# A two-layer-block transformer kernel: 37 products of two constants taken out of TensorE's program at three borders between stages

## The chip, the cores and the metric

The kernel runs on one core of one Trainium2 chip. The metric is the device time of one execution in microseconds (us); the time of a kernel is the median of its runs.

## The reference

A first block (norm, chunked attention with relative positions beside a gated short convolution, gates, an MLP with squared ReLU) and then two layers of a second block. All of it is on 512 tokens of 1024 channels in float32. Cut to what the change touches:

```python
def rmsnorm(x, g):
    xf = x.astype(F32)
    y = xf * lax.rsqrt(jnp.mean(xf * xf, axis=-1, keepdims=True) + NORM_EPS)
    return (y * g.astype(F32)).astype(x.dtype)

for layer in range(DEPTH_2):                     # 2 layers
    u = rmsnorm(h, norm_g[layer, 0])
    ...
    y = mixer(u, mem_kv, ...)                    # window attention in layer 0, HGRN2 in layer 1
    h = h + rmsnorm(y, norm_g[layer, 1])
    f = conv_ffn(rmsnorm(h, norm_g[layer, 2]), ffn_w_in[layer], ffn_conv_w[layer],
                 ffn_conv_b[layer], ffn_w_out[layer])
    h = h + rmsnorm(f, norm_g[layer, 3])
```

The three borders are the places where `h + rmsnorm(y, ...)` of one product's output has to be complete before the next product can begin: after layer 0's mixer, after layer 0's `conv_ffn`, and after layer 1's mixer.

## The kernel before, in words

The program is written by hand, one instruction stream for each engine, with semaphores between them. Activations lie with channels on the partitions: 8 tiles of 128 channels, 512 tokens in the columns. Each matrix product is made of three products of parts ("three_passes", L604 to L606): weights and activations are split into a high and a low part (w_hi, w_lo, h_hi, h_lo), and high by high, low by high and high by low are added up in a PSUM bank of 512 columns. The weights stream from memory through a ring of 6 slots; GpSimd splits them.

A stage is one such matrix product (`STAGES` in the program): blocks of 128 output channels, each a sum over the stage's tiles of input channels. A stage with a "lead" runs its first four blocks side by side: step k takes input tile k into all four banks, 12 products with 512 columns a step, so it can begin as soon as the first tile of h is there. `lead_first` (L656, L657, L660) is step 0 of the two ffn_in stages and of b_in, with the four h_lo products put last; `lead_step` is each later step (L604 to L606).

The order of TensorE's work is the order in which the code calls it. Around a border this is `last_block`, for the last of the 8 output blocks of a_out, ffn_out0 and b_out:

- all tiles of the block but three; then the sum over channels of the squares of the seven earlier blocks (`square_sums`, L940, products with one column of the constant ones, into ps_t); then the last three tiles;
- ScalarE squares the last accumulator (L1358), `square_sums` adds it (L940), ScalarE takes the root (rms, L1368), VectorE the reciprocal (rstd, L1866);
- TensorE spreads rstd over the partitions with four products with the constant ident (L981, into ps_o);
- VectorE scales y with it and with the gain (L1871), adds it to x_res (L1882); ScalarE makes h_hi of tile 0 (L1373) and VectorE h_lo (L1837). The eight tiles follow each other, and the next stage's lead takes them in this order.

`turning` (L948) stands in the three holes of that sequence: products of the constants ones and ident, 128 by 128 in float32, into the bank that block 0 of the next stage will start afresh. Their result is used by nobody. `gain_rows` (L955) stands at the third border alone: eight products that lay the gain of the last norm along the rows, read by ScalarE.

```python
            def turning(st, count):
                bank_free(st, 0)
                for _ in range(count):
                    nc.tensor.matmul(banks[st.banks[0]][:, 0:P], const("ones"), const("ident"), start=True, stop=True)
```

Calls of `last_block`: from `mixer_out` with a_out (first border, next stage ffn_in0), from `conv_mlp(0)` with ffn_out0 (second, next b_in), from `mixer_out` with b_out (third, next ffn_in1).

Of the kernel before, what the change touches and what calls it, by code (L numbers as in the profile page):

```python
# [25 lines left out]
P = 128  # L26
# [160 lines left out]
def build(nc, stream, x_in, mem_in, consts_in, rope_in, params_in, masks_in, ext_in, out):  # L187
# [11 lines left out]
    with ExitStack() as ctx:  # L199
# [116 lines left out]
        def const(name, n=P):  # L316
            c = CONST_COLS[name]
            return consts[:, c:c + n]
# [31 lines left out]
        banks = [*acc, *ps_s, ps_o, ps_t]  # L350
# [233 lines left out]
        def _(pe):  # L584
# [3 lines left out]
            def out_free():  # L588

                if n["copied"]:  # L590
                    pe.wait_ge(o_copied, n["copied"])
                if n["o"]:
                    pe.wait_ge(o_taken, n["o"])

            def take_t(sem_, value):

                if t_free:
                    pe.wait_ge(*t_free[0])
                t_free[:] = [(sem_, value)]
# [10 lines left out]
            def bank_free(st, c):  # L610

                if st.before[c] is not None:
                    before, i = st.before[c]
                    pe.wait_ge(before.free, i + 1)
                elif st.name == "conv":
                    pe.wait_ge(stages["v1"].free, c + 3)
                elif st.name == "gate":
                    pe.wait_ge(s_used, n["unit"])
                elif c == BANKS and st.name not in ("a_out", "b_out"):
                    pe.wait_ge(s_used, n["unit"])  # L620
                    out_free()
# [51 lines left out]
            def block_tiles(st, first, end, x_hi, x_lo, cols=T, done=1):  # L673

                for tile in range(first, end):
                    c, k = divmod(tile, st.kt)
                    if k == 0:
                        bank_free(st, c)
                    if tile % SLOT_TILES == 0:
                        pe.wait_ge(split_made, st.first_slot + tile // SLOT_TILES + 1)  # L680
                    three_passes(st, banks[st.banks[c]][:, 0:cols], (st.first_slot + tile // SLOT_TILES) % RING,
                                 tile % SLOT_TILES, x_hi, x_lo, k, cols, done)
# [240 lines left out]
            st = stages["proj"]  # L923
# [13 lines left out]
            def square_sums(src, last):  # L937

                for b in range(BLOCKS):
                    mm = nc.tensor.matmul(ps_t[:, b:b + 1], src[:, b * P:(b + 1) * P], const("ones")[:, 0:1],  # L940
                                          start=False, stop=last and b == BLOCKS - 1)
                return mm

            def turning(st, count):

                bank_free(st, 0)
                for _ in range(count):
                    nc.tensor.matmul(banks[st.banks[0]][:, 0:P], const("ones"), const("ident"), start=True, stop=True)  # L948

            def gain_rows(then, half):  # L950

                lead_block = GAIN_LEADS[half]
                bank_free(then, lead_block)
                for i in range(DT // 2):
                    mm = nc.tensor.matmul(banks[then.banks[lead_block]][:, i * P:(i + 1) * P],  # L955
                                          param("norm_g", 56 + half * DT // 2 + i).to_broadcast([P, P]), const("ident"), start=True, stop=True)
                mm.then_inc(gain_made, 1)

            def last_block(st, x_hi, x_lo, sq, then):

                tiles = st.cbs * st.kt
                block_tiles(st, tiles - st.kt, tiles - 3, x_hi, x_lo)
                n["rms"] += 1
                n["y"] += 1
                take_t(rms_ready, n["rms"])
                pe.wait_ge(y_sq_used, (DT - 2) * n["y"])
                nc.tensor.matmul(ps_t[:, 0:BLOCKS], const("ones"), small["zero"][:].to_broadcast([P, BLOCKS]), start=True, stop=False)
                square_sums(rstd_in, False)
                block_tiles(st, tiles - 3, tiles, x_hi, x_lo)
                if then.name == "ffn_in1":  # L970
                    gain_rows(then, 0)
                else:
                    turning(then, 4)
                pe.wait_ge(y_sq, DT * n["y"])
                square_sums(sq[:, (DT - 1) % 2, :], True).then_inc(y_sum, 1)

                turning(then, 2)
                out_free()
                pe.wait_ge(rms_used, n["rms"])
                for b in range(BLOCKS):  # L980
                    mm = nc.tensor.matmul(ps_o[:, b * P:(b + 1) * P], rstd[:, b:b + 1].to_broadcast([P, P]), const("ident"),  # L981
                                          start=True, stop=True)
                mm.then_inc(y_rstd, 1)
                if then.name == "ffn_in1":
                    gain_rows(then, 1)
                    turning(then, 5)
                else:
                    turning(then, 9)
                n["o"] += 1

            def last_slot(st, s, blocks):
# [48 lines left out]
            def conv_mlp(layer):  # L1040
                st = stages[f"ffn_in{layer}"]
                lead(st, h_hi, h_lo, waits_for(h_ready, n["h"]), halves=4 + 2 * layer)
                block_at(st, BANKS, h_hi, h_lo)
                block_tiles(st, (BANKS + 1) * DT, (BANKS + 1) * DT + DT // 2, h_hi, h_lo)
                summed_norm()
                block_tiles(st, (BANKS + 1) * DT + DT // 2, (BANKS + 2) * DT, h_hi, h_lo)
                for c in range(BANKS + 2, st.cbs):
                    block_at(st, c, h_hi, h_lo)
                n["h"] += DT
                if layer:  # L1050
                    last_blocks()
                    return
                st = stages["ffn_out0"]
                for c in range(st.cbs - 1):
                    if c == 0:
                        products(st, 0, hid_hi, hid_lo, ready=waits_for(hid_ready, 0))
                    else:
                        block_at(st, c, hid_hi, hid_lo)
                last_block(st, hid_hi, hid_lo, ffn_tmp, stages["b_in"])

            def mixer_out(st, x_hi, then, first=BANKS):

                for c in range(first, st.cbs - 1):
                    block_at(st, c, x_hi, o_lo2)
                last_block(st, x_hi, o_lo2, square, then)

            st = stages["a_in"]
# [77 lines left out]
            st = out_st  # L1146
# [9 lines left out]
            st = stages["b_in"]  # L1156
# [155 lines left out]
            st = stages["b_out"]  # L1312
# [1351 lines left out]
```

## Time and profile before

| what | value |
|---|---|
| median of 3 runs | 2361.08 us (2360.51 to 2361.22) |
| the profiled execution, its own time | 2361.0 us |
| its span, first to last instruction | 2359.2 us |
| TensorE busy | 2344.3 us, 99% |
| VectorE, ScalarE, GpSimd busy | 1175.1, 649.6, 1621.3 us |
| TensorE's granted clock, mean | 0.999 |
| reads from memory | 90 GB/s over the span |

### The profile page before, as it was taken

What the parts mean: (1) busy time and instruction counts of PE and PEld (TensorE: products, weight loads), DVE (VectorE), ACT (ScalarE), POOL (GpSimd) and SP (SyncE); (2) the same over time, 40 slices, a digit from 0 to 9 for tenths busy, and PEclk for the clock granted to TensorE, in tenths of its full rate; (3) what the DMA queues carried; (4) which work ended last, traced back from release to release, by engine and by line L of the source; (5) the groups of instructions that cost most, each with busy time, mean ns of one, the idle gap of its engine ahead of it and who ended that gap; (6) DMA issues with size and microseconds to landing.
All of it is one profiled execution on the core that took longest, in us unless ns stands there. A gap on an engine that the chain in (4) does not pass through costs nothing.

```text
span 2359.2 us, 31448 instructions
## 1 busy us (share of the span) xinstructions
PE 2344.3 (99%) x11270; PEld 1915.5 (81%) x11270; DVE 1175.1 (50%) x1967; ACT 649.6 (28%) x1252; POOL 1621.3 (69%) x2223
## 2 busy tenths in 40 slices
PE   9999999999999999999999999999999999999999
PEld 8877778888888888777788888887888888888887
DVE  4336654333301324577358653045888885755501
ACT  3233321002201212455221110025667653111111
POOL 8665558787877877657569887763454447988873
PEclk9999999999999999999999999999999999999999
DMA  5232223332333332222223333322222222333332
GB/s 179 85 105 90 82 80 99 98 98 90 98 98 98 98 120 95 81 73 90 72 83 96 98 98 98 98 82 64 71 72 72 72 63 81 98 96 94 97 98 72
DMA packets 63407, 214.41 MB, mean 91 GB/s; under 512 B 6688, under 2 KB 10912, under 8 KB 63136
## 3 DMA queue, kind: packets, MB, share of 16 engines
q1 hardware_dynamic: 60528, 206.55, 28.3%
q10 hardware_dynamic: 2736, 5.96, 0.7%
q8 instruction: 90, 1.47, 0.3%
q14 instruction: 53, 0.43, 0.1%
HBM read 210.38 MB, written 2.10 MB: 90 GB/s over the span
## 4 chain that ended last, share of the span: by engine, by line
PE 50%; DVE 3%; ACT 1%; issue 0%; POOL 0%; DVEq 0%
PE acc L604 12%; PE acc L606 12%; PE acc L605 12%; PE acc L1006 1%; PE acc L1005 1%; PE acc L1007 1%; PE ps_o L791 1%; PE ps_s L1223 1%; PE ps_s L749 1%; PE ps_s L604 1%; PE ps_s L606 1%; PE ps_s L605 1%; PE ps_s L1212 0%; PE ps_o L1282 0%; PE ps_s L1006 0%; PE ps_s L1007 0%
## 5 line engine op out<-in xcount | busy, mean ns | idle before, releaser
L569 POOL TENSOR_TENSOR w_lo<-w_raw,w_hi 128x256 fp32r<-128x256 f32 (+1 forms) x1532 | 1205.8, 818 | 190.8 <-ACT w_hi L1717 175.8
L563 POOL CAST w_hi<-w_raw 128x512 fp32r<-128x512 f32 x686 | 430.8, 657 | 511.7 <-DMA w_raw<-stream 472.2
L604 PE MATMUL acc<-h_hi,w_hi 128*128 128x512 f32 x1701 | 677.2, 398 | 0.8 <-DVE h_lo L1837 0.7
L606 PE MATMUL acc<-h_hi,w_lo 128*128 128x512 f32 x1701 | 663.8, 390 | 0.0
L605 PE MATMUL acc<-h_lo,w_hi 128*128 128x512 f32 x1701 | 662.8, 390 | 0.0
L604 PEld LDWEIGHTS acc<-h_hi,w_hi 128*128 128x128 f32 x1701 | 320.1, 188 | 68.5 <-issue 2.9
L606 PEld LDWEIGHTS acc<-h_hi,w_lo 128*128 128x128 f32 x1701 | 319.3, 188 | 67.6
L605 PEld LDWEIGHTS acc<-h_lo,w_hi 128*128 128x128 f32 x1701 | 319.9, 188 | 65.1 <-issue 2.2
L1398 ACT ACTIVATE probs<-probs,neg_max 128x256 f32<-128x256 f32 (+5 forms) x160 | 86.9, 547 | 129.1 <-DVE neg_max L1950 129.0
L1915 DVE TENSOR_TENSOR hid_tmp<-acc,rstd_in 128x512 f32<-128x512 f32 x82 | 56.7, 692 | 129.0 <-PE acc L606 126.8
L605 PE MATMUL acc<-u_lo,w_hi 128*128 128x512 f32 x256 | 99.6, 389 | 0.0
L604 PE MATMUL acc<-u_hi,w_hi 128*128 128x512 f32 x256 | 99.6, 389 | 0.0
L606 PE MATMUL acc<-u_hi,w_lo 128*128 128x512 f32 x256 | 99.6, 389 | 0.0
L1560 ACT ACTIVATE ffn_tmp<-ffn_tmp 128x512 f32<-128x512 f32 x44 | 27.9, 633 | 245.9 <-DVE ffn_tmp L2194 245.9
L1893 DVE COPY y_all<-acc 128x512 f32<-128x512 f32 x22 | 15.2, 692 | 151.1 <-PE acc L606 126.5
L605 PE MATMUL acc<-o_lo,w_hi 128*128 128x512 f32 x228 | 88.8, 390 | 0.0
L1966 DVE TENSOR_SCALAR probs<-probs,inv_sum 128x256 f32<-128x256 f32 (+3 forms) x160 | 87.1, 585 | 2.8
L2176 DVE TENSOR_TENSOR x_res<-acc,x_res 128x512 f32<-128x512 f32 x16 | 11.1, 692 | 138.0 <-PE acc L606 138.0
L1542 ACT ACTIVATE u_tmp<-u_tmp 128x512 f32<-128x512 f32 x32 | 20.2, 632 | 210.1 <-DVE u_tmp L2168 210.1
L2168 DVE SCALAR_TENSOR_TENSOR u_tmp<-acc,rstd_in 128x512 f32<-128x512 f32 x31 | 21.4, 692 | 107.1 <-PE acc L606 106.7
L604 PE MATMUL acc<-hid_hi,w_hi 128*128 128x512 f32 x176 | 68.6, 390 | 0.0
L605 PE MATMUL acc<-hid_lo,w_hi 128*128 128x512 f32 x176 | 68.5, 389 | 0.0
(454 smaller groups left out, 3944.1 us busy)
## 6 DMA issues: line engine op xcount, KB each, us to landing
w_raw<-stream SPq DMA_DIRECT2D x384, 512.0 KB, 3.5
toeplitz<-ext_in ACTq DMA_DIRECT2D x16, 256.0 KB, 2.8
out<-x_res SPq DMA_DIRECT2D x8, 256.0 KB, 2.4
x_res<-x_in SPq DMA_DIRECT2D x3, 512.0 KB, 7.6
mem<-mem_in ACTq DMA_DIRECT2D x1, 1024.0 KB, 7.3
consts<-consts_in SPq DMA_DIRECT2D x1, 656.0 KB, 9.5
x_res<-x_in SPq DMA_DIRECT2D x2, 256.0 KB, 5.3
rope<-rope_in ACTq DMA_DIRECT2D x1, 512.0 KB, 8.1
```

What stands on the lines that cost most here:

```text
L563: nc.gpsimd.tensor_copy(hi[:, half], raw[:, half]).then_inc(hi_made, 1)
L569: nc.gpsimd.tensor_tensor(lo[:, part], raw[:, part], f32(hi[:, part]), ALU.subtract).then_inc(low_quarter if not end else split_made if i ...
L604: nc.tensor.matmul(ps, hi, x_hi[:, k, 0:cols], start=(k == 0), stop=False)
L605: nc.tensor.matmul(ps, hi, x_lo[:, k, 0:cols], start=False, stop=False)
L606: mm = nc.tensor.matmul(ps, lo, x_hi[:, k, 0:cols], start=False, stop=(k == st.kt - 1))
L749: nc.tensor.matmul(banks[u.bank][:, u.at:u.at + u.width], u.q, u.k, start=True, stop=True).then_inc(s_ready, 1)
L791: mm = nc.tensor.matmul(ps_o[g[0].out_part:g[0].out_part + rows, g[first].out_cols[0]:g[end - 1].out_cols[1]].rearrange("p (u n) -> p u n" ...
L1005: nc.tensor.matmul(out_, hid_hi[:, k, cols], hi, start=(k == 0), stop=False)
L1398: nc.scalar.activation(part, part, ACT.Exp, scale=-1.0, bias=small["neg_max"][:, b:b + 1], accum_out=small["row_sum"][:, b:b + 1]).then_in ...
L1560: nc.scalar.activation(t_, t_, ACT.Gelu_apprx_tanh).then_inc(gelu_ready, 1)
L1915: step(nc.vector.tensor_tensor(dst, src, by, ALU.mult), st.free)
L1966: step(nc.vector.tensor_scalar(part, part, inverse[:, i:i + 1], None, ALU.mult), pn_ready)
```

## The change

The function `turning` and its five calls are taken out. At the first and second border 4, 2 and 9 of its products go, at the third 2 and 5: 37 in all. Everything else stays, with its order and its waits.

```diff
-            def turning(st, count):
-
-                bank_free(st, 0)
-                for _ in range(count):
-                    nc.tensor.matmul(banks[st.banks[0]][:, 0:P], const("ones"), const("ident"), start=True, stop=True)
...
                 block_tiles(st, tiles - 3, tiles, x_hi, x_lo)
                 if then.name == "ffn_in1":
                     gain_rows(then, 0)
-                else:
-                    turning(then, 4)
                 pe.wait_ge(y_sq, DT * n["y"])
                 square_sums(sq[:, (DT - 1) % 2, :], True).then_inc(y_sum, 1)
 
-                turning(then, 2)
                 out_free()
                 pe.wait_ge(rms_used, n["rms"])
                 for b in range(BLOCKS):
...
                 mm.then_inc(y_rstd, 1)
                 if then.name == "ffn_in1":
                     gain_rows(then, 1)
-                    turning(then, 5)
-                else:
-                    turning(then, 9)
                 n["o"] += 1
```

TensorE's program at the first border, before: the last three products of a_out's last block, then the border, then the first products of ffn_in0 (acc are the accumulator banks, consts holds ones and ident).

```order
L604 MATMUL acc<-o_hi_114,w_hi 128x512
L605 MATMUL acc<-o_lo_113,w_hi 128x512
L606 MATMUL acc<-o_hi_114,w_lo 128x512
L948 MATMUL acc<-consts 128x128 x4
L940 MATMUL ps_t<-consts,square 128x1 x4
L948 MATMUL acc<-consts 128x128 x2
L981 MATMUL ps_o<-consts,rstd 128x128 x4
L948 MATMUL acc<-consts 128x128 x9
L656 MATMUL acc<-h_hi,w_hi 128x512
L657 MATMUL acc<-h_hi,w_lo 128x512
```

The same place in the changed kernel, where L973 is what L981 was:

```order
L604 MATMUL acc<-o_hi_114,w_hi 128x512
L605 MATMUL acc<-o_lo_113,w_hi 128x512
L606 MATMUL acc<-o_hi_114,w_lo 128x512
L940 MATMUL ps_t<-consts,square 128x1 x4
L973 MATMUL ps_o<-consts,rstd 128x128 x4
L656 MATMUL acc<-h_hi,w_hi 128x512
L657 MATMUL acc<-h_hi,w_lo 128x512
```

Nothing has moved but the 15 products that are gone; eight products stand between the last of one stage and the first of the next. The second border differs in the same rows. At the third border, TensorE's program before (params holds the gains):

```order
L606 MATMUL acc<-o_hi_heads,w_lo 128x512
L955 MATMUL acc<-consts,params 128x128 x4
L940 MATMUL ps_t<-consts,square 128x1 x4
L948 MATMUL acc<-consts 128x128 x2
L981 MATMUL ps_o<-consts,rstd 128x128 x4
L955 MATMUL acc<-consts,params 128x128 x4
L948 MATMUL acc<-consts 128x128 x5
L656 MATMUL acc<-h_hi,w_hi 128x512
```

and in the changed kernel, where L950 is what L955 was:

```order
L606 MATMUL acc<-o_hi_heads,w_lo 128x512
L950 MATMUL acc<-consts,params 128x128 x4
L940 MATMUL ps_t<-consts,square 128x1 x4
L973 MATMUL ps_o<-consts,rstd 128x128 x4
L950 MATMUL acc<-consts,params 128x128 x4
L656 MATMUL acc<-h_hi,w_hi 128x512
```

The eight products of gain_rows stay where they were.

## Rows read from the trace of the kernel before

**Rows 1.** Page, parts 1 and 4: busy time, and the chain that ended last

```profile
PE 2344.3 (99%) x11270; PEld 1915.5 (81%) x11270; DVE 1175.1 (50%) x1967; ACT 649.6 (28%) x1252; POOL 1621.3 (69%) x2223
...
PE 50%; DVE 3%; ACT 1%; issue 0%; POOL 0%; DVEq 0%
```

**Rows 2.** TensorE's longest waits: us in total, times, longest us

```profile
PE acc L1023 <- ACT y_all L1801: 2.1, 1, 2.1
```

**Rows 3.** Timeline, first border: start, us, engine, line, operation, [idle before <-releaser]

```profile
1196.10 0.39 PE L606 MATMUL acc<-o_hi,w_lo 128*128 128x512 f32 x1
...
1196.33 1.05 PE L948 MATMUL acc<-consts 128*128 128x128 f32 x8
1196.53 0.60 ACT L1358 ACTIVATE square<-acc 128x512 f32<-128x512 f32 x1 [3.65 <-PE acc L606]
...
1197.22 1.01 PE L940 MATMUL ps_t<-consts,square 128*128 128x1 f32 x8
...
1198.09 0.69 PE L948 MATMUL acc<-consts 128*128 128x128 f32 x4
...
1198.89 1.13 PE L981 MATMUL ps_o<-consts,rstd 128*128 128x128 f32 x8
...
1199.85 2.17 PE L948 MATMUL acc<-consts 128*128 128x128 f32 x18
...
1201.57 0.72 ACT L1373 ACTIVATE h_hi<-x_res,params 128x512 fp32r<-128x512 f32 x1 [3.04 <-DVE x_res L1882]
...
1202.39 0.47 PE L656 MATMUL acc<-h_hi,w_hi 128*128 128x512 f32 x1 [0.36 <-issue]
...
1205.61 0.50 PE L604 MATMUL acc<-h_hi,w_hi 128*128 128x512 f32 x1 [0.25 <-DVE h_lo L1837]
```

**Rows 4.** Line L948: duration ns min/median/max, first and last start

```profile
L948 PE MATMUL acc<-consts x74: 270/275/357, 1196.3 to 1987.8; 128*128 128x128 f32 x74
```

**Rows 5.** Timeline, second border

```profile
1567.65 2.17 PE L948 MATMUL acc<-consts 128*128 128x128 f32 x18
...
1570.19 0.47 PE L656 MATMUL acc<-h_hi,w_hi 128*128 128x512 f32 x1 [0.36 <-issue]
```

**Rows 6.** Timeline of TensorE in the tail

```profile
2351.51 0.39 PE L1007 MATMUL ps_t<-w_lo,hid_hi 128*128 128x512 f32 x1
...
2354.04 1.66 PE L1023 MATMUL acc<-consts,y_all 128*128 128x128 f32 x8 [2.15 <-ACT y_all L1801]
```

**Rows 7.** Stretches, first border and tail: us; busy by engine; PEclk, DMA, GB/s

```profile
1196.50:1202.30 5.80, 5.42 (x46) 5.07 (x45) 3.04 (x5) 1.59 (x4) 0.00 (x0) 1.00 0.30 93
...
2354.00:2354.20 0.20, 0.16 (x2) 0.19 (x3) 0.00 (x0) 0.00 (x0) 0.00 (x0) 1.00 0.00 0
2354.20:2354.40 0.20, 0.20 (x3) 0.20 (x3) 0.00 (x0) 0.00 (x0) 0.00 (x0) 0.90 0.00 0
2354.40:2354.60 0.20, 0.20 (x3) 0.20 (x2) 0.00 (x0) 0.00 (x0) 0.00 (x0) 0.50 0.00 0
```

**Rows 8.** A pause in b_in: its stretch (PEclk third from the end), and timeline

```profile
1693.50:1697.00 3.50, 2.21 (x15) 1.81 (x14) 3.12 (x5) 3.07 (x6) 0.00 (x0) 1.00 0.49 150
...
1694.60 1.05 PE L1212 MATMUL ps_s<-hg_qd_both,hg_grow_f 128*128 128x128 f32 x8
1696.94 0.33 PE L1248 MATMUL ps_t<-consts,hg_block_k 128*128 128x128 f32 x1 [1.29 <-ACT ffn_tmp L1671]
```

**Rows 9.** The kernel's start: line L912, then TensorE's timeline in two stretches

```profile
L912 PE MATMUL ps_o<-columns x48: 273/282/583, 0.9 to 8.7; 128*128 128x128 f32 x48
...
1.27 4.99 PE L912 MATMUL ps_o<-columns 128*128 128x128 f32 x23
...
5.75 2.96 PE L912 MATMUL ps_o<-columns 128*128 128x128 f32 x24
```

**Rows 10.** Timeline, third border

```profile
1985.87 1.06 PE L955 MATMUL acc<-consts,params 128*128 128x128 f32 x8
...
1988.40 0.47 PE L656 MATMUL acc<-h_hi,w_hi 128*128 128x512 f32 x1 [0.36 <-issue]
```

## The prediction, made before the changed kernel was run

> **What bounds the kernel now.** I read the page's busy shares and its chain of waits first. TensorE has work on record for 99% of the span, and of the shares that the chain names TensorE has 50% and all other engines together 4% [rows 1]. So whatever delays TensorE at a border is added to the end, if no later wait of TensorE swallows it. I looked through the list of waits for one that would: the longest wait of TensorE is 2.1 us, and it is the one in the tail [rows 2]. Nothing between the first border and the tail has that size.
>
> Then the timeline at the first border, where attention's output projection ends and ffn_in0 begins [rows 3]. The reader is to see a chain that TensorE only serves in pieces. The last product with 512 columns starts at 1196.10. ScalarE squares its accumulator (1196.53 to 1197.13), TensorE sums the squares over the channels with products of one column (from 1197.22), the root and the reciprocal follow, TensorE spreads the result over the partitions (L981, 1198.89 to 1200.02), VectorE scales and adds, ScalarE makes h_hi (1201.57 to 1202.29), and at 1202.39 the next stage's products begin. The products of two constants (L948) stand in the three holes between these: 8, 4 and 18 records, two for each product. All 37 of the three borders make 74 records [rows 4]. The second border reads the same, 367.8 us later, with the same 18 records before its first L656 [rows 5].
>
> Last, TensorE's granted clock. It is 1.00 all through the borders, and over the whole span it falls once: in the tail [rows 7].
>
> **The change, part by part.**
>
> *The products themselves.* 30 records leave each of the first two borders, 14 leave the third. Are they on the path? In the first hole the removed records seem to end as the square does: L940's product starts 0.09 us after the square's end at 1197.13. Elsewhere a product follows the operation that it waits for by about as much: L656 starts 0.10 us after h_hi's end at 1202.29 [rows 3]. In the third hole the last of 18 records ends at 2.17 us after 1199.85, thus at 1202.02, 0.27 us before h_hi. So the path runs beside them, and removing them gives nothing: I take 0. The bounds are 0.3 us of loss or gain for all three borders together, about 0.1 a border, the size of the gaps just named. Nobody waits for these products: they signal no semaphore, and the one wait they contain (for the accumulator of block 0) stands again ahead of the first L656.
>
> *What stands idle now.* Without them TensorE has, between the product at 1196.10 and the one at 1202.39, only 8 records of one column and 8 of L981. The last hole, 1200.02 to 1202.39, is 2.4 us of standing still [rows 3].
>
> *What standing still does to the clock.* The tail shows it. There the last product with 512 columns starts at 2351.51, TensorE is idle for 2.15 us, and 8 records of 128 columns begin at 2354.04 [rows 6]. In the slice from 2354.20 to 2354.40 the granted clock leaves 1.00, and from 2354.40 on it is 0.50, the lower of its two levels, 1.2 in place of 2.4 GHz [rows 7]. That is some 2.7 us after TensorE's last full product, with 8 short records under way. The first two borders now have 6.1 us, from 1196.33 to 1202.39, in which 16 short records are all that TensorE does, and the last 2.4 us of it are empty. On the other side there is one stretch that held the clock at 1.00 with a pause: 1.29 us of idle time after 8 records of 128 columns [rows 8]. The changed borders, with a pause of 2.4 us, are nearer to the tail. I take it that the clock falls at borders one and two, before or at the beginning of the next stage's products.
>
> The Trainium skill speaks against that: "TensorE: Matmul & The Clock Gate", section "Why this matters for your kernels", advises no gaps without work over about 3 us between bursts. By that rule no hole here is long enough and the change would cost nothing. This case's tail disagrees, with its 2.15 us.
>
> *What the lower clock costs.* The kernel's start shows both levels on the same instruction, 128 columns of float32: 23 records in 4.99 us, and a little later 24 records in 2.96 us [rows 9]. Without the last record's own length of about 0.4 us that is 4.6/22 = 0.21 us a record against 2.56/23 = 0.11 us. So 0.47 of each microsecond at the lower clock is lost. How long does it last? The start is the only rise in the trace: products run from 0.89 without a pause, and the faster spacing begins at about 6.0, 5.1 us later [rows 9]. (The clock column reads 1.00 there too; its records begin only with this first change, so the spacing is what counts.) The nearest other reaction of the clock is the fall in the tail, 2.7 us. Between 2.7 and 5.1 us I take 4.4: nearer to the start's value, as that is a rise and the other a fall, but below it, since the lead products need not begin at the same point as they did there. A border loses 0.47 x 4.4 = 2.07 us.
>
> From that comes off what TensorE waits anyway: 0.25 us before the second step's first product (L604 at 1205.61, waiting for h_lo) [rows 3]. A slower first step fills it. Later steps of this stage have no idle time on TensorE, so nothing more is absorbed: 2.07 - 0.25 = 1.82 us.
>
> If the clock falls early, L981 runs slow as well, and it is on the path. 8 records take 1.66 us in the tail, where most of them ran at the lower clock [rows 6], against 1.13 us at the border [rows 3]: 0.5 us in full, 0 if the clock falls later. In the tail it fell 2.7 us after the last full product, which at the border is 1198.8, just where L981 begins. I take 0.1, since the border is not idle up to there as the tail is; the bounds are 0 and 0.5.
>
> *The third border* keeps 16 records of products that carry gains (L955): 8 in the first hole, 8 in the last, where they end at 1986.93. The stretch without TensorE is then 1.5 us, to 1988.40 [rows 10]. That is close to the 1.29 us which the clock survived [rows 8], so I take 0 here, and a fall as a rival.
>
> **Sum.** Two borders at 1.82 + 0.1 = 1.92 us: +3.8 us. The profiled execution took 2361.0 us by its own time, so 2364.8 us; the median shown is 0.08 us above it, so 2364.9 us. The bounds of this case: 2.7 us at the lower clock give 0.47 x 2.7 - 0.25 = 1.0 a border, +2.0 us; 5.1 us with L981 slow give 2.15 + 0.5 = 2.65 a border, +5.3 us. The case lies between 2363.1 and 2366.4 us.
>
> **Rivals.**
>
> *The third border falls too; slower beyond doubt.* Place: the 1.5 us before L656 at 1988.40, and the hole before L981, 0.7 us as at the first border [rows 3]. Price: the same 1.92 us, so +5.8 us, 2366.9 us. It decides as soon as the 1.5 us, with the gain products' 8 records ahead of it, is too thin for the clock. For it: the tail's 2.15 us is only 0.65 us more. Against it: the pause of 1.29 us that held, and that each hole here keeps products on one side.
>
> *Only one border falls, or both only for a moment.* If the chip counts the one-column products and L981 as work, the stretch without work is only the 2.4 us hole, barely above the tail's 2.15 us, and one of the two borders may get by: +1.9 us, 2363.0 us. For it: TensorE had also done nothing since 2351.74 in the tail, which is emptier than 1196.33 to 1200.02 here. Against it: the border's thin stretch lasts 6 us in all.
>
> *The clock stays up*, the skill's rule as a mechanism of this kernel: all holes (0.9, 0.7 and 2.4 us) are too short, and the lower clock in the tail belongs to the program's ending and not to the pause. Then only the 0.1 us gaps are left: 2361.1 us. For it: no fall anywhere but in the tail. Against it: no other pause over 1.3 us exists, so it was never tried.
>
> *It gets faster.* The removed records would have to hold up the y chain. Their price is bounded by the gaps above to 0.3 us, so it takes something that the trace does not show.
>
> **How the numbers follow.** A measurement of this kernel can tell about 0.2% from no change, here 4.7 us, so the border lies at 2365.8 us. Chances: two borders fall 0.53, of which 0.16 lies above 2365.8; three fall 0.19, of which 0.18 lies above; one falls 0.15; none 0.10; faster 0.03. That makes slower 0.34, same 0.37 + 0.01 + 0.15 + 0.10 = 0.63, faster 0.03. The range leaves out the faster case, most of "none" and the top of the three-border case: 2361.7 to 2367.4 us.
>
> **What would show it.** In the changed kernel's profile: the granted clock at 0.50 in slices around the first L656 of borders one and two and 1.00 at the third; L656 to L660, 12 products, taking about 5 us in place of 3.0 us; L604's wait for h_lo (0.25 us) gone there; L940's and L656's distances to ScalarE's ends unchanged. The prediction is wrong if the clock reads 1.00 at all borders, if a border loses over 3 us, or if the y chain from the last full product to the first L656 is longer than 6.3 us by more than 0.5 us.

## The result, and the profile of the changed kernel

| | median | runs |
|---|---|---|
| before | 2360.60 us | 20 runs, 2360.01 to 2361.28 |
| changed | 2364.59 us | 20 runs, 2363.86 to 2365.92 |

The ratio is 1.0017, with a 95% interval of 1.0011 to 1.0023: slower by 4.0 us, where +3.8 us was forecast, and inside the range. The two sets of runs don't overlap. This is just under the 0.2% that the prediction said a measurement can tell from no change; with 20 runs on each side it was told apart all the same.

The profiled execution of the changed kernel took 2364.07 us, with a span of 2362.3 us and a mean granted clock of 0.996. Its first border reads like this (timeline: start, us, engine, line, operation; L973 is what L981 was, L1347 what L1358 was):

```profile
1195.62 0.39 PE L606 MATMUL acc<-o_hi,w_lo 128*128 128x512 f32 x1
1196.05 0.60 ACT L1347 ACTIVATE square<-acc 128x512 f32<-128x512 f32 x1 [3.64 <-PE acc L606]
...
1196.70 1.05 PE L940 MATMUL ps_t<-consts,square 128*128 128x1 f32 x8 [0.69 <-ACT square L1347]
...
1198.41 1.13 PE L973 MATMUL ps_o<-consts,rstd 128*128 128x128 f32 x8 [0.66 <-DVE rstd L1855]
...
1201.91 0.76 PE L656 MATMUL acc<-h_hi,w_hi 128*128 128x512 f32 x1 [2.37 <-issue]
...
1202.47 0.63 PE L657 MATMUL acc<-h_hi,w_lo 128*128 128x512 f32 x1
...
1207.16 0.63 PE L604 MATMUL acc<-h_hi,w_hi 128*128 128x512 f32 x1
...
1208.27 0.40 PE L604 MATMUL acc<-h_hi,w_hi 128*128 128x512 f32 x1
```

It answers to [rows 3], and is best read in two halves. Up to L656 the holes show as idle time (0.69, 0.66 and 2.37 us), and the way from the last full product to L656 is 1201.91 - 1195.62 = 6.29 us, as it was before (1202.39 - 1196.10). So the removed products neither held up the chain nor helped it. After L656 the products come 0.43 us apart in place of 0.23 us, and a record lasts 0.63 us in place of 0.39 us, until 1208. The next stage's second step (L604) begins 5.25 us after L656 in place of 3.22 us, and without the wait for h_lo that [rows 3] has.

The clock around the fall, and over the first three steps of each border's lead (stretches: us; busy time and records of TensorE, its weight loads, VectorE, ScalarE, GpSimd; granted clock; DMA share; GB/s). A stretch of the second kind runs from the first L656 to the first product of step 3:

```profile
1201.91:1213.07 11.16, 11.16 (x37) 8.91 (x37) 10.39 (x14) 5.37 (x9) 7.93 (x11) 0.72 0.12 33
1572.05:1582.48 10.43, 10.43 (x36) 8.44 (x37) 9.69 (x13) 5.36 (x9) 7.20 (x10) 0.78 0.12 38
1991.69:2000.48 8.79, 8.57 (x36) 6.76 (x37) 8.19 (x11) 4.64 (x8) 5.56 (x8) 1.00 0.17 44
1200.91:1201.11 0.20, 0.00 (x0) 0.00 (x0) 0.17 (x2) 0.02 (x1) 0.00 (x0) 1.00 0.00 0
1201.11:1201.31 0.20, 0.00 (x0) 0.00 (x0) 0.20 (x1) 0.20 (x1) 0.00 (x0) 0.79 0.00 0
1201.31:1201.51 0.20, 0.00 (x0) 0.00 (x0) 0.20 (x1) 0.20 (x1) 0.00 (x0) 0.50 0.00 0
```

The same three stretches of the kernel before:

```profile
1202.39:1211.20 8.81, 8.56 (x36) 6.76 (x37) 8.21 (x11) 4.13 (x7) 5.58 (x8) 1.00 0.15 38
1570.19:1579.00 8.81, 8.58 (x36) 6.76 (x37) 8.21 (x11) 4.13 (x7) 5.58 (x8) 1.00 0.14 43
1988.40:1997.23 8.83, 8.62 (x36) 6.76 (x37) 8.23 (x11) 4.65 (x8) 5.60 (x8) 1.00 0.14 41
```

The clock falls in the pause, at about 1201.2. The reader is to see that the loss is the difference of the first numbers: 11.16 - 8.81 = 2.35 us at the first border, 10.43 - 8.81 = 1.62 us at the second, none at the third, where the clock stays at 1.00. Together 3.97 us, where the medians differ by 4.0 us. That the two agree so closely is in part luck, since the two profiled executions differ by only 3.1 us (2364.07 against 2361.0 us). Along the program the difference reads so: the last full product of the stage is 0.48 us earlier than in the kernel before at the first border (1195.62 against 1196.10), 1.87 us later at the second (1565.77 against 1563.90), which is 2.35 us between the two, and 3.30 us later at the third (1985.41 against 1982.11), which is 1.43 us more where 1.62 us were lost. Those 0.2 us came back between the borders, and the 0.48 us were there before any change in the program; both are of the size by which the runs of one kernel differ. The last 0.2 us go in the tail, where the kernel before had slow records in its profile and the changed kernel had none (see e7).

### The profile page after: what moved, and what is told of

Read it like the earlier page. It is cut to its first block, busy times and chain, and to the rows that moved or that the text cites. A ratio compares the mean times of both kernels' runs of the same rounds, so it can differ in the third digit from the quotient of the medians.

```text
span 2362.3 us, 31300 instructions
## 1 busy us (share of the span) xinstructions
PE 2340.1 (99%) x11196; PEld 1910.2 (81%) x11196; DVE 1170.9 (50%) x1967; ACT 649.8 (28%) x1252; POOL 1625.0 (69%) x2223
## 4 chain that ended last, share of the span: by engine, by line
PE 50%; DVE 2%; ACT 1%; issue 0%; POOL 0%; DVEq 0%
PE acc L604 12%; PE acc L606 12%; PE acc L605 12%; PE acc L995 1%; PE acc L996 1%; PE acc L994 1%; PE ps_o L791 1%; PE ps_s L1212 1%; PE ps_s L749 1%; PE ps_s L604 1%; PE ps_s L605 1%; PE ps_s L606 1%; PE ps_s L1201 0%; PE ps_o L1271 0%; PE ps_s L995 0%
## 5 line engine op out<-in xcount | busy, mean ns | idle before, releaser
L604 PE MATMUL acc<-h_hi,w_hi 128*128 128x512 f32 x1701 | 676.9, 398 | 0.4 <-DVE h_lo L1826 0.2
L604 PEld LDWEIGHTS acc<-h_hi,w_hi 128*128 128x128 f32 x1701 | 320.2, 188 | 67.0 <-issue 2.9
L604 PE MATMUL acc<-u_hi,w_hi 128*128 128x512 f32 x256 | 99.6, 389 | 0.0
L604 PE MATMUL acc<-hid_hi,w_hi 128*128 128x512 f32 x176 | 68.6, 390 | 0.0
```

The source lines that it names most:

```text
L604: nc.tensor.matmul(ps, hi, x_hi[:, k, 0:cols], start=(k == 0), stop=False)
```

## The experiments

The theory (A): TensorE's granted clock falls where it streams too little at a border, and the next stage's first products then run at half pace; the removed products did nothing else. The rival (B): what costs is that TensorE stands still or its queue runs empty, and any instruction in the holes would help. All times are medians; the comparison is the kernel before, run beside each group of experiments (2360.57 to 2360.62 us). Of each execution the record has the mean granted clock too, to three digits; 0.001 of it is 4.7 us at the lower clock (twice 0.001 of 2360 us), and a fall at the very end of the program is in it. For the kernel before it reads 0.999 or 1.000 in every one of the 88 runs beside the experiments, for the changed kernel 0.995 or 0.996 in all 30.

**e1: something in the holes, but nearly no columns.**

```diff
-                    nc.tensor.matmul(banks[st.banks[0]][:, 0:P], const("ones"), const("ident"), start=True, stop=True)
+                    nc.tensor.matmul(banks[st.banks[0]][:, 0:1], const("ones"), const("ident")[:, 0:1], start=True, stop=True)
```

> The 37 products of constants stay, with their loads of the constant ones, but each streams one column in place of 128. Theory A (the lower clock comes because TensorE streams too few columns there): the clock falls at borders one and two as in the changed kernel, +3.5 to +4.5 us against the kernel before. Theory B (what costs is that TensorE stands still, or that its queue is empty, so any instruction in the hole helps): 0, within 0.5 us, clock 1.00 at all three borders. If the products now last longer than the holes, L656 begins later than 0.1 us after h_hi's end, and that part is told apart by its wait.

Measured: 2366.59 us (7 runs, 2366.26 to 2367.96), +6.0 us, above the expected 3.5 to 4.5 us and worse than with nothing in the holes. First border, TensorE's timeline, and two stretches of it (granted clock third from the end):

```profile
1195.81 0.39 PE L606 MATMUL acc<-o_hi,w_lo 128*128 128x512 f32 x1
1196.04 0.95 PE L948 MATMUL acc<-consts 128*128 128x1 f32 x8
1196.88 1.05 PE L940 MATMUL ps_t<-consts,square 128*128 128x1 f32 x8
1197.80 0.58 PE L948 MATMUL acc<-consts 128*128 128x1 f32 x4
1198.59 1.85 PE L981 MATMUL ps_o<-consts,rstd 128*128 128x128 f32 x8 [0.21 <-DVE rstd L1866]
1200.23 3.84 PE L948 MATMUL acc<-consts 128*128 128x1 f32 x18
1203.93 0.77 PE L656 MATMUL acc<-h_hi,w_hi 128*128 128x512 f32 x1
```

```profile
1200.40:1203.90 3.50, 3.50 (x19) 3.50 (x18) 3.21 (x5) 1.21 (x2) 0.00 (x0) 0.50 0.02 5
1196.00:1198.70 2.70, 2.49 (x22) 2.40 (x21) 0.87 (x2) 0.86 (x2) 0.00 (x0) 1.00 0.43 129
```

TensorE is busy almost without a break, 3.50 us of 3.50 in the hole before L656, and the clock is at 0.50 there; it fell between 1198.80 and 1198.90. So busy time and weight loads did not hold the clock here, where the same 37 products with 128 columns each did; the edit took nothing away but the columns. Rival B is out. What e1 costs beyond the changed kernel has two visible parts: the clock fell as L981 ran, which now takes 1.85 us on the chain in place of 1.13 us, and the 18 slow records (3.84 us) outlast the hole, so that L656 starts 1.2 us after h_hi's end (1202.71) in place of 0.1 us. Together it starts 8.12 us after the last full product in place of 6.29 us; at the second border the same way is 7.61 us. These are 1.83 + 1.32 = 3.15 us on top, as much as this profiled execution (2367.72 us, one of the three longer ones of the seven) lies above the changed kernel's median; the median of e1 is 2 us above it. At the third border, with its gain products, the clock stayed at 1.00 here too.

**e2, e3 and e10: one border at a time.** The calls of `turning` carry a condition on the next stage's name; for e2:

```diff
-                else:
+                elif then.name != "ffn_in0":
                     turning(then, 4)
...
-                turning(then, 2)
+                if then.name != "ffn_in0":
+                    turning(then, 2)
...
-                else:
+                elif then.name != "ffn_in0":
                     turning(then, 9)
```

e10 has "b_in" in its place, and e3 leaves the 2 and the 5 products of the third border out.

> Only the first border is without the products (4, 2 and 9 of them); the second and the third are as in the kernel before. Theory A: one fall, half of the change: +2.0 us (1.5 to 2.7), with the clock at 1.00 at the other two borders. Rival: the first loss lets later work slip into place and the two borders are not additive: under +1 or over +3 us.

> Only the third border is without its 7 products; the 8 products that carry gains stay there. Theory A with the third border as in the changed kernel's profile: clock 1.00 there, 0 within 0.3 us. Rival: in some executions the clock falls there too, so the median is the same but the slowest executions are 1 to 2 us above the kernel before.

> Only the second border is without the products. Additive borders: the change (+4.0) less the first border alone (+1.86) gives +2.1 us (1.6 to 2.6), one fall. Rival: the borders share something, and the second alone costs under 1 or over 3 us.

| kernel | median, 11 runs each | against before | lowest to highest |
|---|---|---|---|
| e2, first border empty | 2362.44 us | +1.86 us | 2361.47 to 2363.97 |
| e10, second border empty | 2362.80 us | +2.23 us | 2362.22 to 2364.08 |
| e3, third border empty | 2360.42 us | -0.16 us | 2360.07 to 2361.01 |

The sum is 3.9 us, against 4.0 us for the three together: the borders are additive, and the third is worth nothing. In none of the 11 runs of e3 is there a sign of a fall: the slowest took 2361.01 us, and the mean granted clock is 0.999 or 1.000 in all. In e2 and e10 it is 0.998 or 0.997 in all. The 95% intervals of the single ratios (e2: 1.0000 to 1.0018, e10: 1.0001 to 1.0019) are wide beside these differences; what carries the reading is that not one run of e2 or e10 lies below 2361.4 us, and none of the 29 and 27 runs of the kernel before beside them above it.

**e4 and e5: which hole?**

e4 leaves out the 4 and the 2 products of the first two holes, e5 the 9 (and 5) of the last:

```diff
e5
                 if then.name == "ffn_in1":
                     gain_rows(then, 1)
-                    turning(then, 5)
-                else:
-                    turning(then, 9)
```

> The 9 (third border: 5) products in the last hole, ahead of the next stage, stay; the 4 and 2 of the first two holes go. If the standing still of 2.4 us alone brings the fall: 0 within 0.3 us and clock 1.00. If all of the thin stretch counts: falls in part of the executions, +0.5 to +2 us, some executions like the kernel before and some 2 us or more above it.

> The 4 and 2 products of the first two holes stay, the last hole (2.4 us of standing still) is empty, at the third border the 5 last ones are gone too. If that pause alone brings the fall: as the changed kernel, +3.5 to +4.5 us. If the whole thin stretch counts: between, +1 to +3 us, with executions that differ by 2 us and more. If no hole alone matters: 0.

e4: 2360.97 us (2360.49 to 2363.25), +0.4 us. Its profile shows no fall at a border, but that is one execution. In six of the 11 the mean granted clock is 0.998 or below (0.997 in the slowest), which none of the 29 runs of the kernel before beside them shows. That is 7 us or more at the lower clock; the fall in the tail alone makes about 5 us in the profile of the kernel before, from 2354.3 to its end. These six took 2360.79 to 2363.25 us (median 2361.6), the five others 2360.49 to 2360.97 us. So with the first two holes empty the clock falls in a part of the executions although the last hole is filled, as the second of the two expectations had it. At which border it falls, and how late, is not shown: no profile of such a run was taken.

e5: 2362.65 us (2361.49 to 2363.71), +2.0 us, half of the change, and 0.998 or 0.997 in all 11 runs. It has a fall at both borders, a later one (TensorE's timeline, first border, and the stretch as defined above):

```profile
1198.84 1.13 PE L981 MATMUL ps_o<-consts,rstd 128*128 128x128 f32 x8
1202.35 0.47 PE L656 MATMUL acc<-h_hi,w_hi 128*128 128x512 f32 x1 [2.37 <-issue]
1202.65 0.42 PE L657 MATMUL acc<-h_hi,w_lo 128*128 128x512 f32 x1
1202.88 0.61 PE L656 MATMUL acc<-h_hi,w_hi 128*128 128x512 f32 x1
```

```profile
1202.35:1212.21 9.86, 9.86 (x36) 7.96 (x37) 9.13 (x13) 5.04 (x9) 6.64 (x9) 0.83 0.14 37
```

The first two products still run at full pace and the clock falls at the third, after the pause has ended. So the pause of 2.37 us is enough for a fall even behind filled holes; what empty first holes add is that the fall comes earlier and lasts longer. Neither hole alone decides: with the last hole empty each of 11 executions had a fall, with the first two empty about half of them.

**e6 and e9: how much is enough?** e6 has 4 products in place of 9 in the last hole. e9 gives borders one and two the pattern that the gain products make at the third, 4 in the first hole, none in the second, 4 in the last, and has no `turning` at the third.

```diff
e9
-                turning(then, 2)
...
-                    turning(then, 5)
                 else:
-                    turning(then, 9)
+                    turning(then, 4)
```

> As the kernel before, but 4 products in place of 9 in the last hole of borders one and two (about 1.2 us of the 2.4 us hole stay idle). If the clock needs the hole nearly full: +1 us or more. If a half-filled hole is as good, as the third border suggests, where 8 records and a pause of 1.5 us did not bring the fall: 0 within 0.3 us, clock 1.00.

> Borders one and two get the filling that the third border keeps in the changed kernel: 4 products in the first hole, none in the second, 4 in the last; the third border is without its 7. If the 16 records of the gains are why the third border held: 0 within 0.3 us, clock 1.00 at all three borders. If the third border held by luck: +0.5 to +2 us and falls in part of the executions.

e6: 2360.63 us (2360.14 to 2361.08), 0. e9: 2360.15 us (2359.72 to 2360.57), -0.4 us, within what its interval (0.9990 to 1.0008) can't tell from zero. e9's first border, and then the granted clock over it (third from the end):

```profile
1198.27 1.13 PE L980 MATMUL ps_o<-consts,rstd 128*128 128x128 f32 x8 [0.66 <-DVE rstd L1864]
1199.23 1.06 PE L948 MATMUL acc<-consts 128*128 128x128 f32 x8
1201.77 0.47 PE L656 MATMUL acc<-h_hi,w_hi 128*128 128x512 f32 x1 [1.48 <-issue]
```

```profile
1195.71:1201.70 5.99, 3.92 (x33) 3.67 (x31) 3.06 (x5) 1.61 (x4) 0.00 (x0) 1.00 0.28 88
```

A pause of 1.48 us passes, as at the third border, and all 11 runs of e6 and of e9 read 0.999 or 1.000. 16 of the 37 products do what all 37 did. Set beside e4, it matters more where they stand than how many there are: 4 and 4 (e9) held the clock in each of 11 executions, 9 in the last hole alone (e4) did not. (e9 ran on another chip than e4; the kernel before reads the same on both.)

**e7 and e8: the same products where the trace has its own fall.** The tail of the kernel before has a pause of 2.15 us and a fall [rows 6, 7]. e7 fills it; e8 does so too and drops the third border's products.

```diff
                         last_slot(st, s, [b])
...
+                for _ in range(TAIL):
+                    nc.tensor.matmul(banks[st.banks[0]][:, 0:P], const("ones"), const("ident"), start=True, stop=True)
                 last_turn(BLOCKS - 1)
```

> The kernel before with 8 products of constants in the tail's 2.15 us pause, into a bank that has been read. Theory A: the clock no longer falls before the last 8 records (L1023), which take 1.05 us in place of 1.66 us: -0.3 to -0.7 us, less in the median because the fall does not meet those records in each execution. Rival: the products end after the wait and delay the records: 0 or above.

> The tail filled as above, the products kept at borders one and two and gone at the third. By e3 (0 at the third border) the sum is that of the filled tail alone: -0.3 to -0.7 us. Rival: the third border has a fall in some executions: slowest runs 1 to 2 us above the others.

e7: 2360.65 us (2359.89 to 2361.58), 0; e8: 2360.71 us (2359.88 to 2361.45), +0.1 us. The expected gain of 0.3 us and more did not come. The tail of the kernel before (three lines), then e7's:

```profile
2354.04 1.66 PE L1023 MATMUL acc<-consts,y_all 128*128 128x128 f32 x8 [2.15 <-ACT y_all L1801]
2354.89 0.69 DVE L2227 TENSOR_TENSOR x_res<-acc,x_res 128x512 f32<-128x512 f32 x1 [0.89 <-PE acc L1023]
2355.74 0.69 DVE L2227 TENSOR_TENSOR x_res<-acc,x_res 128x512 f32<-128x512 f32 x1 [0.16 <-PE acc L1023]
```

```profile
2352.47 1.95 PE L1040 MATMUL ps_s<-consts 128*128 128x128 f32 x16
2354.78 1.06 PE L1024 MATMUL acc<-consts,y_all 128*128 128x128 f32 x8 [0.37 <-ACT y_all L1804]
2355.44 1.49 DVE L2230 TENSOR_TENSOR x_res<-acc,x_res 128x512 f32<-128x512 f32 x2 [0.71 <-PE acc L1024]
```

The 8 records take 1.06 us, where the kernel before has 1.66 us. Two things make the gain small. VectorE's two additions follow the records half by half: they end 2.39 us after the first record's start before and 2.15 us in e7, so of the 0.6 us on TensorE 0.24 us reach the next engine. And the slow records are not the rule. Eleven profiles here have the unfilled pause of 2.15 us; in six (the changed kernel, e1, e2, e3, e6, e10) the eight records take 1.06 us as well, the clock falling after them or not at all before the end, and in five (the kernel before, e4, e5, e9, e11) 1.29 to 1.94 us. So e7's 1.06 us in one profile shows nothing by itself. What speaks for the filling is the mean granted clock: 1.000 in all 22 runs of e7 and e8, 0.999 in 25 of the 32 of the kernel before. The gain that this leaves, some 0.1 us on average by estimate (0.24 us in about half of the executions), is too small to measure here. No version here beats the kernel before by more than can be measured.

**e11: the changed kernel a second time.** The edit is that of the change.

> The changed kernel again, for a second profile of it. Time +3.7 to +4.3 us against the kernel before, two falls. The time at the lower clock is expected to differ between the profiles (6.1 and 4.6 us with products running at the two borders of the first) and the loss of each border with it, at 0.47 us for each us, less what TensorE waited for before.

Measured: 2364.14 us (10 runs, 2363.57 to 2364.86), +3.6 us, just outside the expected 3.7 to 4.3 us on the low side. Its profile shows what the first did not, a fall early enough to meet the rstd products on the chain at the second border (timeline, then a stretch):

```profile
1568.00 1.78 PE L973 MATMUL ps_o<-consts,rstd 128*128 128x128 f32 x8 [0.66 <-DVE rstd L1855]
1569.82 0.76 DVE L1860 SCALAR_TENSOR_TENSOR ps_s<-y_all,params,ps_o 128x512 f32<-128x512 f32 x1 [1.96 <-PE ps_o L973]
```

```profile
1568.40:1572.10 3.70, 1.38 (x7) 1.08 (x6) 2.21 (x3) 0.76 (x2) 0.00 (x0) 0.50 0.06 25
```

L973 takes 1.78 us in place of 1.13 us, and all that follows is 0.65 us later. In return less of the lead runs slow: its stretch is 9.64 us.

## Why the prediction was right, point by point

*The products are beside the path: 0.* Right. The way from the last full product to L656 is 6.29 us with them and without them, at all three borders; it is longer only where the fall comes early (e11's second border: 6.94 us). That one is over the 6.8 us which the prediction named as a sign of being wrong; it is L973 that is slow there, the term for L981 below, and not the missing products.

*The clock falls at borders one and two, and the third holds.* Right, in both profiles of the changed kernel and in e2, e5 and e10. Its main evidence was weaker than it looked, though: the tail's pause of 2.15 us meets a fall in time to slow the next records in only five of eleven profiles (see e7), and it was luck that the one on hand was of the five. The rivals are settled with it. "The third border falls too": e3's 11 runs and every profile speak against it, and e9 shows that the pattern of its gain products is enough at the two other borders. "Only one border falls": all 30 runs of the changed kernel read 0.995 or 0.996, where one empty border gives 0.997 or 0.998 (e2, e10); and e1 contradicts the assumption behind it for the one-column products, which did not hold the clock. "The clock stays up" rests on the Trainium skill ("TensorE: Matmul & The Clock Gate", section "Why this matters for your kernels"), which advises against gaps without work of over about 3 us. e5 has no pause longer than 2.37 us, behind filled holes, and falls. Taken as a limit, as the prediction took it for this rival, the advice would have it stay up; the measurement decides.

*What the lower clock costs.* Seven stretches in which it fell, set against their 8.81 us before (the second border of e5 reads as its first; e1 is left out, as L656 itself was delayed there, but its first border fits too: 10.67 us at 0.76, a loss of 1.86 us where the last column would have 1.9 us). Time at the lower clock is twice (1 - granted clock) times the stretch:

| kernel, border | stretch, us | granted clock | at the lower clock, us | loss, us | 0.47 x that - 0.55 |
|---|---|---|---|---|---|
| changed, first | 11.16 | 0.72 | 6.2 | 2.35 | 2.4 |
| changed, second | 10.43 | 0.78 | 4.6 | 1.62 | 1.6 |
| e2, first | 10.54 | 0.77 | 4.8 | 1.73 | 1.7 |
| e10, second | 10.94 | 0.74 | 5.7 | 2.13 | 2.1 |
| e5, first | 9.86 | 0.83 | 3.4 | 1.05 | 1.0 |
| e11, first | 10.26 | 0.79 | 4.3 | 1.45 | 1.5 |
| e11, second | 9.64 | 0.85 | 2.9 | 0.83 | 0.8 |

Four of the rows behind this table (e2, e10, and the two borders of e11), as the stretches of the trace have them:

```profile
1202.21:1212.75 10.54, 10.54 (x37) 8.47 (x38) 9.81 (x13) 5.37 (x9) 7.32 (x10) 0.77 0.13 38
```

```profile
1570.06:1581.00 10.94, 10.94 (x37) 8.74 (x37) 10.21 (x13) 5.36 (x9) 7.71 (x11) 0.74 0.13 34
```

```profile
1202.26:1212.52 10.26, 10.26 (x37) 8.34 (x37) 9.53 (x13) 5.37 (x9) 7.03 (x10) 0.79 0.14 40
1572.16:1581.80 9.64, 9.64 (x37) 7.91 (x37) 9.01 (x12) 4.80 (x9) 6.41 (x9) 0.85 0.15 42
```

The rate of 0.47 us for each us holds in all seven. The prediction took it from the start's two spacings, and there one is too small: it takes 0.4 us off as the last record's own length, where [rows 9] has a median of 0.28 us, so 0.117 us in place of 0.11 us and a rate of 0.44; the first of those 24 records were still at the slower spacing, so the two nearly cancel. The lead's own spacings, 0.43 us against 0.227 us, give 0.47 directly. The choice of 4.4 us was a guess between two bounds, and that it came so near to the average was luck. Over the four borders of the changed kernel's two profiles the time is 6.2, 4.6, 4.3 and 2.9 us, 4.5 us on average. But 6.2 us lies above the 5.1 us that was called the upper bound: a single rise in a trace bounds nothing. The border's loss stayed under the bound of 2.65 us all the same, because more was absorbed (0.55 us in place of 0.25 us) and L973 was not slow there.

*What TensorE waits anyway, 0.25 us.* Too small: 0.55 us. The idle time of 0.25 us in [rows 3] is counted from the end of the last record, but a record ends some 0.16 us after the next one could have begun at the pace of 0.23 us. L656 to L604 is 3.22 us. The second product starts 0.31 us after the first, and eleven more at 0.227 us make 2.80 us, so 0.42 us are free. The rest, 0.13 us, lies in the 24 products of steps 1 and 2, which take 8.81 - 3.22 = 5.59 us in the kernel before, 0.233 us each in place of 0.227 us. Most of it is the first of them: after the wait for h_lo the next product starts 0.33 us later and not 0.23 us, and where that wait is gone, so is this. Both starts in the kernel before, against [rows 3]:

```profile
1202.70 0.39 PE L657 MATMUL acc<-h_hi,w_lo 128*128 128x512 f32 x1
1205.94 0.40 PE L605 MATMUL acc<-h_lo,w_hi 128*128 128x512 f32 x1
```

So the prediction was wrong to say that nothing more is absorbed after the first step.

*L981 slow: 0.1 us.* 0, 0, 0.05 and 0.65 us at the four borders, 0.2 us on average, and 0.65 us at most where 0.5 us was the bound.

So two terms were too small in opposite directions. With the measured ones a border costs 0.47 x 4.5 - 0.55 + 0.2 = 1.8 us, against 1.92 us in the prediction, and two of them 3.6 us: e11's +3.6 us, a little under the 4.0 us of the first measurement. That +3.8 us lies between the two owes something to luck; the mechanism doesn't.

*The chances.* A result within 0.2% had 0.63; it came out at 0.17%, close to the bound, as the sum did (0.16%).

## What to carry to other kernels

Where TensorE serves a chain of other engines and streams little for some microseconds, look up the granted clock over the first products of the *next* stage, not only over the pause; most of the loss stands there. A few products of constants between the last and the next stage's products held the clock here, at no cost as long as they ended before the wait did. With 128 columns each they held it, with one they did not (e1). About 1 us of them in the hole of 2.4 us was enough with as much in the first hole (e6, e9); all in the last hole was not (e4). Look at the clock of every execution and not of the profiled one alone: it is what shows the falls of e4, and it would have shown how unsteady the one in the tail is. Before paying for more, price the loss: here 2 us a border, 0.17% of this kernel in all, as it comes twice.

## What the runs showed of the hardware that had not been expected

- TensorE with 3.50 us of busy time in 3.50 us, nearly all of it products of one column with their weight loads, ran at the lower clock (e1). The busy share in a profile does not tell the clock.
- Weight loads slow down with the clock too: the one-column records, with a weight load busy in 3.50 us of 3.50 us, start 0.21 us apart at the lower clock (18 in the 3.70 us from 1200.23 to 1203.93) and 0.105 us apart at the upper one (8 in the 0.84 us from 1196.04 to 1196.88) (e1).
- The clock can fall after the pause is over: in e5 at the third product of the new stage, 0.5 us after it began. The granted clock up to the end of the pause does not show it.
- The same program spent 6.2 and 4.3 us of products at the lower clock at its first border in two executions, 4.6 and 2.9 us at its second. The pause of 2.15 us in the tail slowed the records behind it in five of eleven profiles. One profile gives the mechanism, but not its mean price: the changed kernel's runs spread over 2.06 us, those of the kernel before over 1.27 us.
